# A search split between VectorE and ScalarE: five sets at two bits a tile, and the steps of the sample spread over other pairs

## The reference, cut to what matters

```python
def index_select(qi, wi, ki, q_pos, k_top):
    s = jnp.einsum('bthd,bsd->bths', qi, ki).astype(jnp.float32) * IDX_DIM ** -0.5
    score = jnp.einsum('bths,bth->bts', jax.nn.relu(s), wi.astype(jnp.float32) * IDX_HEADS ** -0.5)
    score = jnp.where(admissible, score, -jnp.inf)
    vals, idx = lax.top_k(score, k_top)
    return idx, vals > -jnp.inf

def sparse_attend(q, ks, vs, valid):
    s = jnp.einsum('bthd,btkhd->bthk', q, ks).astype(jnp.float32) * HEAD_DIM ** -0.5
    p = jax.nn.softmax(jnp.where(valid[:, :, None, :], s, -jnp.inf), axis=-1)
    return jnp.einsum('bthk,btkhd->bthd', p, vs)
...
    u = x @ params['w_in'][l]      # z, xbc, dt, q, k, v, qi, ki, wi, glu
...
    y_ssd, ssm_new = ssd_scan(xs, dt, a, bm, cm, ssm_prev.astype(jnp.float32))
    y_att = attend(q, k, v, qi, ki, wi).reshape(bsz, t, ATT_WIDTH)
    c, cc_conv_new = causal_dwconv(gl, cc_conv_prev, params['cc_conv_w'][l], params['cc_conv_b'][l])
```

## Time and profile before

| | us |
|---|---|
| median of 3 runs | 3915.68 (3914.45 to 3916.64) |
| the profiled execution | 3910.14 |
| its span | 3908.3 |
| PE busy in the span | 3335.0 (85%) |
| DVE busy | 1942.7 (50%) |
| ACT busy | 1193.1 (31%) |
| POOL busy | 635.6 (16%) |
| mean granted clock of TensorE, share of full | 0.908 |

### The profile page before, as it was taken

One profiled execution on the slowest core, in us unless ns is written; L12 is line 12 of the kernel. 1 busy time (PEld: TensorE's weight loads), 2 busy tenths in 40 slices (PEclk: granted clock), 3 DMA queues, 4 the chain that ended last, 5 costly groups with the idle time before them and its releaser, 6 DMA issues.

```text
span 3908.3 us, 51642 instructions
## 1 busy us (share of the span) xinstructions
PE 3335.0 (85%) x19286; PEld 2670.2 (68%) x19286; DVE 1942.7 (50%) x3096; ACT 1193.1 (31%) x2127; POOL 635.6 (16%) x651
## 2 busy tenths in 40 slices
PE   5899777866789999999868997787668899999995
PEld 2444346623689999999834443565338899999995
DVE  4477873341375435334435879633315754344335
ACT  3226513332242112212222473142322422122113
POOL 0000000001004334333100000000110233333331
PEclk8999888857799999999989998897669999999998
DMA  2200003303401111111021010142043011111111
GB/s 98 55 27 27 27 21 110 104 17 90 131 9 36 55 44 38 52 47 38 26 80 46 27 33 27 35 123 77 6 133 87 22 39 46 52 44 39 55 36 57
DMA packets 169892, 206.57 MB, mean 53 GB/s; under 512 B 61025, under 2 KB 138146, under 8 KB 168738
## 3 DMA queue, kind: packets, MB, share of 16 engines
q1 hardware_dynamic: 143138, 185.36, 16.0%
q10 hardware_dynamic: 26496, 17.84, 1.6%
HBM read 187.17 MB, written 15.96 MB: 52 GB/s over the span
## 4 chain that ended last, share of the span: by engine, by line
PE 61%; DVE 19%; ACT 8%; SPq 5%; issue 4%; DMA 2%; POOL 0%; ACTq 0%; DVEq 0%; POOLq 0%
PE PS L731 40%; PE PS L712 5%; DVE WORK L1660 4%; DVE WORK L1852 3%; DVE MIX L1660 2%; SPq L413 2%; SPq L414 2%; PE PS L744 2%; PE PS L816 2%; ACT X L1297 2%; ACT WORK L1426 1%; PE PS L924 1%; DMA RING<-cache_k 1%; PE PS L770 1%; DVE WORK L1624 1%
## 5 line engine op out<-in xcount | busy, mean ns | idle before, releaser
L731 PE MATMUL PS<-WORK_parts,WHIGH_parts 128*128 128x352 f32 x4224 | 869.9, 328 | 35.2 <-POOL WORK_parts L698 17.7
L712 PE MATMUL PS<-X,RING 128*128 128x512 f32 (+1 forms) x2016 | 684.5, 502 | 129.1 <-DMA RING<-w_in 65.6
L731 PEld LDWEIGHTS PS<-WORK_parts,WHIGH_parts 128*128 128x128 f32 x4224 | 724.5, 191 | 38.9 <-issue 20.6
L731 PE MATMUL PS<-WORK_parts,RING_parts 128*128 128x352 f32 x3168 | 691.4, 327 | 0.0
L712 PEld LDWEIGHTS PS<-X,RING 128*128 128x128 f32 x2016 | 343.7, 196 | 470.8 <-issue 401.7
L731 PEld LDWEIGHTS PS<-WORK_parts,RING_parts 128*128 128x128 f32 x3168 | 545.3, 190 | 0.0
L1660 DVE SCALAR_TENSOR_TENSOR WORK<-WORK,VEC 128x1072 f32<-128x1072 f32 (+2 forms) x272 | 525.6, 1932 | 9.7
L1243 ACT ACTIVATE WORK<-PS 128x32 f32<-128x32 f32 (+11 forms) x412 | 190.5, 513 | 960.8 <-PE PS L731 579.7
L478 POOL TENSOR_TENSOR RING_parts<-RING,WHIGH_parts 128x1024 fp32r<-128x1024 f32 (+2 forms) x184 | 372.0, 2022 | 489.6 <-ACT WHIGH_parts L1243 489.2
L731 PE MATMUL PS<-X_parts,WHIGH_parts 128*128 128x352 f32 x2016 | 434.4, 323 | 0.0
L731 PEld LDWEIGHTS PS<-X_parts,WHIGH_parts 128*128 128x128 f32 x2016 | 344.3, 188 | 0.0
(11 more groups left out here) (318 smaller groups left out, 3741.8 us busy)
## 6 DMA issues: line engine op xcount, KB each, us to landing
RING<-w_up SPq DMA_DIRECT2D x88, 512.0 KB, 3.6
RING<-cache_k SPq DMA_DIRECT2D x200, 128.0 KB, 2.2
RING<-cache_v SPq DMA_DIRECT2D x192, 128.0 KB, 2.1
RING<-w_in SPq DMA_DIRECT2D x46, 512.0 KB, 3.7
RING<-w_down SPq DMA_DIRECT2D x80, 256.0 KB, 2.7
RING<-cache_v ACTq DMA_DIRECT2D x64, 128.0 KB, 2.5
RING<-cache_k ACTq DMA_DIRECT2D x56, 128.0 KB, 2.5
yT<-X SPq DMA_DIRECT2D x5, 1408.0 KB, 5.5
```

The lines of the kernel that those rows point to most:

```text
L712: mm = pe.matmul(job_psum(n, w, first=first), stationary(k), moving(k)[:, first:first + w], start=k == 0, stop=k == k_tiles - 1)
L731: mm = pe.matmul(thirds(n)[:, third, :], a, x[:, third * THIRD:(third + 1) * THIRD], start=k == 0 and part == 0, stop=k == tiles - 1 and p ...
```

## The change

1. Block 3 (512 columns) joins the blocks that ScalarE counts (`SCANNED` has five), and the scratch space `SCAN_ASIDE` gets the widths of the blocks.
2. `BITS_OF_JOB`: two bits behind every job from GATE to K and one behind K+1, where before two or three stood behind GLU to Z+3. The amounts of `spend` behind a job are others, too, and in the chunks 2 and 4 instead of 4, 1 and 7.
3. The sample's choices stand three in a pair in pairs 0 to 2, the turns three in a pair in pairs 4 to 6, `weigh_fresh` in pair 7, and the values three in a pair from pair 7 on. `exp_sample` moves from pair 5 to pair 3, `largest_of_sample` from the ninth block to the sixth, and ScalarE issues its value pages behind `copy_turned` instead of ahead of it.

```diff
--- before.py
+++ after.py
@@ -146,12 +146,23 @@
 NORM_TILES = {"cc": 2, "rms": 4}
 NORM_BASE = {"cc": 0, "rms": 2}
 BLOCKS = [(i, h) for i in range(NCHUNK) for h in range(ATT_HEADS)]
+TURNED_AT, WEIGHED_AT = 4, 7
+
+
+def turns_of_pair(p):
+    return range(max(3 * (p - TURNED_AT), 0), min(max(3 * (p - TURNED_AT) + 3, 0), 9))
+
+
+def values_of_pair(p):
+    return range(max(3 * (p - WEIGHED_AT), 0), min(max(3 * (p - WEIGHED_AT) + 3, 0), STREAM))
+
+
 SCORED = [(i, t, k, min(512, (i + 1) * P - k)) for i in range(2, NCHUNK) for t in range(2) for k in range(0, (i + 1) * P, 512)]
-SCANNED = (4, 5, 6, 7)
+SCANNED = (3, 4, 5, 6, 7)
 SCAN_SCALE = 2.0 ** 24
-BITS_OF_JOB = {T_GLU: 2, T_GATE + 1: 3, T_GLU + 1: 3, T_Z: 3, T_Z + 1: 3, T_Z + 2: 3, T_Z + 3: 2}
-BITS_OF_JOB.update({_j: 2 for _j in range(T_XBC, T_GATE)})
-LAST_BITS = T_Z + 3
+BITS_OF_JOB = {_j: 2 for _j in range(T_XBC, T_K + 1)}
+BITS_OF_JOB[T_K + 1] = 1
+LAST_BITS = T_K + 1
 assert sum(BITS_OF_JOB.values()) == 31
 
 
@@ -276,8 +287,8 @@
         WCOL = spare[:, n_qis + n_wmat:n_qis + n_wmat + 8]
 
         at[0] = VTOK_AT
-        SCAN_ASIDE = [view(SEQ // 2).bitcast(BF16) for _ in SCANNED]
-        assert at[0] <= qi_at
+        SCAN_ASIDE = [view((i + 1) * P // 2).bitcast(BF16) for i in SCANNED]
+        assert at[0] <= VTOK_AT + (NCHUNK + 1) * 256
         at[0] = WORK_SIZE - 5 * len(SCANNED)
         SCAN_SUM, SCAN_LIMIT, SCAN_TRIED, SCAN_ONE, SCAN_NEXT = (view(len(SCANNED)) for _ in range(5))
 
@@ -1153,17 +1164,15 @@
 
                 def sample_steps(p):
 
-                    if p < 9:
-                        for m in range(2 * p, min(2 * p + 2, 9)):
+                    if p < TURNED_AT:
+                        for m in range(3 * p, min(3 * p + 3, 9)):
                             yield lambda m=m: add_choice(m)
-                    if 6 <= p < 12:
-                        for m in range(2 * (p - 6), min(2 * (p - 6) + 2, 9)):
-                            yield lambda m=m: turn_sample(m)
-                    if p == 10:
+                    for m in turns_of_pair(p):
+                        yield lambda m=m: turn_sample(m)
+                    if p == WEIGHED_AT:
                         yield weigh_fresh
-                    if p >= 11:
-                        for g in range(5 * (p - 11), min(5 * (p - 11) + 5, STREAM)):
-                            yield lambda g=g: weigh_values(g)
+                    for g in values_of_pair(p):
+                        yield lambda g=g: weigh_values(g)
 
                 n_pairs = len(BLOCKS) // 2
                 for p in range(n_pairs + 2):
@@ -1514,18 +1523,17 @@
                     for n in (2 * p, 2 * p + 1):
                         if n < len(BLOCKS):
                             exp(n)
-                    if p == 5:
+                    if p == TURNED_AT - 1:
                         exp_sample()
-                    if 6 <= p < 11:
-                        for m in range(2 * (p - 6), min(2 * (p - 6) + 2, 9)):
-                            copy_sample(m)
-                    if p >= 11:
-                        for g in range(5 * (p - 11), min(5 * (p - 11) + 5, STREAM - NSLOT)):
-                            act.wait_ge(v_used, g + 1)
-                            load_pages(act, layer, ("value", g + NSLOT), (3,))
+                    for m in turns_of_pair(p):
+                        copy_sample(m)
                     if p >= 1:
                         copy_turned(2 * p - 2)
                         copy_turned(2 * p - 1)
+                    for g in values_of_pair(p):
+                        if g + NSLOT < STREAM:
+                            act.wait_ge(v_used, g + 1)
+                            load_pages(act, layer, ("value", g + NSLOT), (3,))
                 stage.end()
 
 
@@ -1969,7 +1977,7 @@
                             ssd_convolved.append(True)
                         if j == LAST_BITS:
                             aside.append(chosen)
-                        spend(12 if T_K <= j < T_V else 30 if j >= T_V else 2, aside)
+                        spend(4 if j < T_K else 0 if j == T_K else 5 if j < T_Q else 11 if j < T_V else 6, aside)
                 stage.end()
 
 
@@ -2003,7 +2011,7 @@
                     dve.tensor_tensor(XW[rows, :, :], XDT[rows, :, :],
                                       WS[rows, ch, :].unsqueeze(2).broadcast_to([L, SSD_HEADS, HEAD]), ALU.mult
                                       ).then_inc(ssd["taken"], 1)
-                    spend(4, aside)
+                    spend(2, aside)
                     dve.wait_ge(ssd["scores"], ch + 1)
                     dve.tensor_copy(BTOK[rows, :], bank(1, P, rows))
                     dve.wait_ge(ssd["decay"], ch + 1)
@@ -2016,7 +2024,6 @@
                     if not last:
                         if ch == 0:
                             dve.wait_ge(pool_step, 3)
-                        spend(1, aside)
                     dve.wait_ge(ssd["y"], ch + 1)
                     if not last:
                         step.then_wait(dve.tensor_tensor(HP[:, :, :], HP[:, :, :],
@@ -2031,7 +2038,7 @@
                     y = MIX[:, 0:4, cols]
                     gated = step.mark(dve.tensor_tensor(y, y, YT[:, :, 0:L], ALU.mult))
                     if not last:
-                        spend(7, aside)
+                        spend(4, aside)
                     else:
 
                         for b in range(DEC_BATCH):
@@ -2115,9 +2122,9 @@
                     mask(n)
                     if n >= 1:
                         invert(n - 1)
-                    if n < 9:
-                        add_choice(n)
-                    if n == 9:
+                    for m in range(3 * (n // 2) + 2 * (n % 2), min(3 * (n // 2) + 2 + n % 2, 9)):
+                        add_choice(m)
+                    if n == 6:
                         largest_of_sample()
                     if n >= 8 and n % 4 == 0:
                         take_out(n // 4 - 2)
```

## The result

The changed kernel took 3825.51 us (median of 4 runs, 3816.51 to 3832.36), the kernel before 3915.2 beside it: a ratio of 0.9769, 95% interval 0.9748 to 0.979. That is faster by 2.3%, 90 us. The forecast said 3833, its own range 3818 to 3848. The profiled execution took 3816.51, its span 3814.7, where it was 3910.14 and 3908.3 before: 93.6 less.

The account below looks back on a forecast made before the run. The prediction took VectorE's serial work to bound the projections and SyncE's issue to pace the attention's value stream. Projections, chunks and attention summed to 2 x (23.5 + 0 + 18) = 83 us less, so 3833, range 3818 to 3848.

Parts of the forecast that it names:

- The third rival: Attention: the value stream isn't paced by issue; the stage gives 24 us a layer, 95 in all, time 3821; chance 0.14.
- Projections, -23.5 a layer: Input projections: fewer counts on VectorE, two bits a tile and later ties save 23.5 us a layer; bounds 12 to 28.
- The walk over the tiles: Projections, tile by tile from GATE to V+1: K rotated at 493.6 instead of 531.6, chunks starting at 590 instead of 613.27.
- The forecast's lower bound, 12 for the saved counts alone: Projections: if only the counts taken off VectorE move the stage, it gets 12 us a layer shorter.
- Chunks, 0: State-space chunks: one set of ties (6.5 us) left in chunk 0 costs 0; without cover, 6.5 a layer.
- Attention, -18 a layer: Attention pairs: first value read 17.7 us earlier, stream still 108 long; stage 18 a layer less, bounds 12 to 24.
- ScalarE's hand-overs (first): Projections: evacuations queue behind two bits on ScalarE, 17 tiles lose 0.7 us each; gain 11.5 a layer, time 3857; chance 0.19.
- The attention (second): Attention gives only 8 us a layer, as pairs 3 to 6 grow or late pairs run 12; time 3853; chance 0.12.
- The clock (fourth): Projections: waits before most tiles keep TensorE at 1.2 GHz for part of each; slower, time 3960; chance 0.03.
- The fifth: No change: time given back in the chunks (6.5 us) and lost behind V+1; needs 41 a layer; chance 0.02.

## Why the prediction was right, and where its terms were off

**Bound.** That VectorE's serial work in the projections and SyncE's issue in the attention bound the kernel held. The second was a reading of one row and is now shown: half the bytes leave the row as it was, two thirds of the issues shorten the stage by 17. Moving one page in three groups from SyncE to ScalarE saves some 6 us a layer, and moving one in every group loses 8. The rule of the Trainium skill that the prediction weighed (DMA: Bandwidth & Descriptors, section "Issuing engines are not separate DMA queues") says that several issuers save only the time of initiating, usually small beside the DMA itself. That it is small does not agree with these runs: an issue took 1.19 us beside 2.1 from issue to landing. The third rival is refuted, though its time, 3821, is closer to the measured one than mine.

**Projections, -23.5 a layer: measured -27.1 and -25.4.** The walk over the tiles held nearly to the microsecond. Counted from the stage's start (201.90 then, 203.90 now): the XBC wait ends at 111.1 for a forecast 111.8, the last bit is settled at 284.7 for 285.6, K is rotated at 290.8 for 291.7. The step that was off is the way from K's rotation to the mean's product: 27.6 us (28.7 before), where I had counted 31.4, the old way and some 3 for Q's slow tile. That price was about right. Q waited 15.44, its tile took 17.48, and it ended at 501.23, 2.7 behind VectorE's rotation of K (498.55). So K+1's product started 6.35 behind the start of that rotation, where before it was 3.99. What I put at nothing is the rest of the way, 21.3 us for 24.7. Before, TensorE had stood idle 20.60 us ahead of K+1's product, its granted clock was 0.50 there (the lower level), and the products of K+1 and Q took 4.02 and 3.73. Now no wait stands there, the clock is 1.00 and they take 2.10 each, which gives back some 3.5.

```profile
556.79 3.73 PE L712 MATMUL PS<-WORK,CONST 128*128 128x512 f32 x6 [1.39 <-DVE WORK L1678]
```

That row is Q's product before. Everything behind it is some 4 earlier than forecast: V+1 at 352.4 for 357.1, the chunks at 384.3 for 388.1.

The parts of it: the fifth set brings about 4, the new budgets 8.0 against the old ones; if they add, the remaining 14 or so belong to the bits spread two a tile, which were not run alone. The forecast's lower bound, 12 for the saved counts alone, was sized too high: the set brought nothing in the XBC and Z tiles.

**Chunks, 0: measured 0.** Layer 0 has 2.9 more, layer 1 2.2 less; over the sixteen stages with one set of ties the mean is 207.6, over the six without any 208.1. The one set stands where it was forecast, in chunk 0, at 592.63, and its 6.5 us do not show in the stage.

**Attention, -18 a layer: measured -23.3 and -17.1.** Over twelve stages of six kernels with these pairs the mean is 190.8, over four with the old pairs 211.9: 21 less. In layer 0 the first value came 23.6 earlier, not 17.7. I had counted 40.1 for the pairs 7 to 10, less 15.4 for the turns and 7 for `largest_of_sample` with its exp. Both deductions were too large. TensorE's wait for the sample's exp was already there before, in pair 5; in pair 3 it is 5.2 longer. First the row before, then the changed kernel's:

```profile
863.93 0.88 PE L1083 MATMUL PS<-CONST,WORK 128*128 128x128 f32 x3 [6.51 <-ACT WORK L1243]
```

```profile
837.42 0.66 PE L1094 MATMUL PS<-CONST,WORK 128*128 128x128 f32 x2 [11.74 <-ACT WORK L1252]
```

And the nine turns, from the first turn of a pair to the step behind them, take 14.9 us in three pairs; pair 6 had 3.6 of this before, so 11.3 are added ahead of the first value and not 15.4. 40.1 less 5.2 and 11.3 is 23.6; the smaller shifts, of the choices and of `weigh_fresh`, cancel. The run with the reductions behind the mask shows that their place ahead of it, the reason that I gave for the 7, costs 1 us at most. That the stream then takes 108 us as before was right (108.3). In layer 1 the first value came 22.1 earlier (75.9 into the stage for 98.0), but from it to the end of the last weighing are 109.8 us where before had 104.8. SyncE's row is alike in both, 98.95 and 98.83 us; 4.4 of the 5 lie behind its last issue, from which to the end of the last weighing are 8.9 us for 4.5. What makes that end vary is not settled. With the same attention the stage took from 184.9 to 193.8, the shortest with its first value 3.9 earlier than the changed kernel's, at a granted clock of 0.69 in the first 27 us for 0.56.

**Sum.** By the terms as measured, 2 x (26.3 + 0 + 21) = 95; the profiled executions differ by 93.6, the medians by 90. The forecast's 83 was low for two reasons: TensorE's pace behind the wait that went away was put at nothing, and the sample's steps in the early pairs were priced too high.

**Rivals.** ScalarE's hand-overs (first) did not stretch the tiles: from the fourth XBC tile on the waits are 2.29, 1.48 and three of 0.16 or less, then none up to K. (Bits stand behind 16 tiles, not 17 as that rival says; its time hardly changes.) The attention (second) gave more than twice 8. The clock (fourth) rose a little, 0.919 for 0.908; only three tiles behind waits took clearly longer, 17.48 to 18.05. The fifth, time given back in the chunks and behind V+1, did not come: the chunks kept their length and V+1 starts 32.9 us earlier in the stage.

## What to carry to other kernels

A queue's row may be a pace: ask whether waits stand inside it, count its issues, and check by halving the bytes and by dropping issues; spread issues only as far as the other engine's own chain has room. When work is moved ahead of a waiting step, ask what the later step needs: a cost that stands on the path to it in either order is not a cost of the move. When a long wait goes away, price also what the engine behind it gets back in pace. And serial work of unequal urgency (here ties, needed two stages later) belongs behind everything that frees a bank, in a stage where its engine idles, even if a little of it shows there.

## What the runs showed of the hardware

An issue of a page held SyncE 1.19 us for 128 KB and 1.17 us for 64 KB (84 in 99.89 and in 98.49). With full pages and 84 issues the same row took 98.5 to 99.9 over the kernels, so the bytes make no difference that shows. ScalarE took 0.88 us each for three in a row (2.63) and 1.01 for six (6.04). The transfers, with the same issues and half the bytes, landed in a median 1.8 instead of 2.1 us.

I had not expected the chunks' length, with one set of ties or none, to vary from 205.3 to 210.8 between layers and kernels, which is more than 24.6 us of added VectorE work changed its mean. The granted clock goes with it: 0.84 to 0.86 in the stages under 206.2 us, 0.82 or 0.83 in those of 209 and more. In pair 2 of layer 1's attention a choice's two products took 2.07 us in the changed kernel, at a granted clock of 0.50, and 1.13 in the kernel with all ties in the chunks, at 0.83.
